# Five pairs of gate tiles instead of four by seven products, and fewer gate steps among the attention units

## What is computed

```python
h = rms_norm(x, g_mix)
proj = h @ w_in                     # A q|k|v, B q|k|v, gate_A, gate_B
y_a = chunk_band_relbias_attention(qa, ka, va, rel_table) @ w_branch_a   # 8 heads
y_b = sliding_window_sink_gqa(rope(qb), rope(kb), vb, sinks) @ w_branch_b  # 8 heads, 2 for keys
g_a, g_b = split(sigmoid(gate_logits + b_gate))   # gate_logits: the last 2 * 1024 columns of proj
x = x + (g_a * y_a + g_b * y_b) @ w_out
x = x + swiglu(rms_norm(x, g_ffn))
```

## Time and profile before

| | |
|---|---|
| median of 3 runs | 2745.28 us (2744.36 to 2747.64) |
| the profiled execution | 2747.8 us |
| its span, first to last instruction | 2745.9 us |
| granted TensorE clock, mean | 0.992 |
| layer 0: projection stage, about | 0 to 293 us |
| layer 0: attention units, about | 299 to 550 us |
| layer 1: attention units, about | 1650 to 1901 us |

### The profile page before, as it was taken

The page is one execution under the profiler, slowest core; times in us unless marked ns, Lnnn a source line. Parts: engine busy times, 40 slices in busy tenths (PEclk is TensorE's granted clock), DMA queues, the critical chain, the costliest instruction groups (busy, mean ns, idle before and its releaser), DMA issues. The chain is left out here.

```text
span 2745.9 us, 37502 instructions
## 1 busy us (share of the span) xinstructions
PE 2688.3 (98%) x13328; PEld 2259.6 (82%) x13328; DVE 1933.4 (70%) x3589; ACT 1173.7 (43%) x2413; POOL 251.5 (9%) x390
## 2 busy tenths in 40 slices
PE   8999999999989999999999999999999999999998
PEld 7788889888878888888778888988887788888887
DVE  6766666654587877767997666666446877786687
ACT  5222577742433333344552227776324333333444
POOL 0000301055200000000000002111450000000000
PEclk8999999999999999999999999999999999999999
DMA  2333433153223222376423334322530322333843
GB/s 96 142 119 105 147 94 94 47 187 132 85 92 115 96 92 104 115 238 195 145 90 116 119 120 132 94 92 75 188 131 29 125 93 103 112 115 114 273 127 123
DMA packets 182295, 330.37 MB, mean 120 GB/s; under 512 B 16992, under 2 KB 62304, under 8 KB 181856
## 3 DMA queue, kind: packets, MB, share of 16 engines
q1 hardware_dynamic: 171968, 301.24, 33.0%
q10 hardware_dynamic: 10144, 26.74, 2.9%
HBM read 235.12 MB, written 92.80 MB: 119 GB/s over the span
## 5 line engine op out<-in xcount | busy, mean ns | idle before, releaser
L1112 PE MATMUL ps<-op_hi,up_hi 128*128 128x512 f32 x1232 | 481.8, 391 | 12.8 <-issue 4.9
L1113 PE MATMUL ps<-op_lo,up_hi 128*128 128x512 f32 x1232 | 480.7, 390 | 0.0
L1114 PE MATMUL ps<-op_hi,up_lo 128*128 128x512 f32 x1232 | 480.6, 390 | 0.0
L1112 PE MATMUL ps<-in_hi,up_hi 128*128 128x512 f32 x728 | 287.9, 396 | 14.9 <-DVE up_lo L2116 11.4
L1751 ACT ACTIVATE up_hi<-up_raw 128x512 fp32r<-128x512 f32 x264 | 165.0, 630 | 294.3 <-PE ps L1114 274.2
L1114 PE MATMUL ps<-in_hi,up_lo 128*128 128x512 f32 x728 | 286.1, 393 | 0.0
L1113 PE MATMUL ps<-in_lo,up_hi 128*128 128x512 f32 x728 | 286.1, 393 | 0.0
L1112 PEld LDWEIGHTS ps<-op_hi,up_hi 128*128 128x128 f32 x1232 | 231.9, 188 | 64.2 <-DVE up_lo L2523 8.5
L1114 PEld LDWEIGHTS ps<-op_hi,up_lo 128*128 128x128 f32 x1232 | 232.1, 188 | 48.6
L1113 PEld LDWEIGHTS ps<-op_lo,up_hi 128*128 128x128 f32 x1232 | 232.1, 188 | 47.9
L1082 POOL CAST w_hi<-w_raw 128x256 fp32r<-128x256 f32 x192 | 82.9, 474 | 1819.0 <-DMA w_raw<-w_lin 1237.9
(11 more groups left out here) (244 smaller groups left out, 5527.9 us busy)
## 6 DMA issues: line engine op xcount, KB each, us to landing
up_raw<-w_gu SPq DMA_DIRECT2D x44, 1024.0 KB, 5.1
act_raw<-ff_saved SPq DMA_DIRECT2D x154, 256.0 KB, 2.8
w_quarter<-w_lin SPq DMA_DIRECT2D x52, 512.0 KB, 4.5
w_raw<-w_lin SPq DMA_DIRECT2D x48, 512.0 KB, 3.9
ff_saved<-ff_block SPq DMA_DIRECT2D x88, 256.0 KB, 2.0
ff_saved<-ff_mix SPq DMA_DIRECT2D x66, 256.0 KB, 2.0
gated<-gates_saved SPq DMA_DIRECT2D x32, 512.0 KB, 4.1
stage<-in_saved SPq DMA_DIRECT2D x48, 256.0 KB, 2.8
```

The costliest lines, as they stand in the source:

```text
L1112: pe.matmul(out, w1, x1, start=first, stop=False, skip_group_check=True)
L1113: pe.matmul(out, w1, x0, start=False, stop=False, skip_group_check=True)
L1114: return pe.matmul(out, w0, x1, start=False, stop=last, skip_group_check=True)
```

## The change

One more pair of gate tiles is computed in the projection stage by seven products: 14 pairs instead of 13 for each layer. Six gate tiles instead of eight are left for plain computing, twelve halves instead of sixteen. Eight steps still stand before the first unit and two halves behind the last, so 10 x 8 - 8 = 72 steps instead of 14 x 8 - 8 = 104 stand among the units. `FILL_A` sums to 22 instead of 26 in group 0 and to 6 instead of 8 in each of the other groups; `FILL_B` is 12, 7, 7 and 6 instead of 14, 14, 14 and 12. Everything else follows from these numbers.

```diff
-IN_GATES = 4
+IN_GATES = 5
 GATE_TILES = 2 * (KT - IN_GATES)
 LIN_TILES = 2 + 4 * GROUPS + 3 * KT + KT
 TILES = GATE_TILES + 2 * KT
@@
-FILL_A = ((3, 3, 3, 2, 2, 2, 2, 1, 1, 1, 1, 1, 1, 1, 1, 1), (1, 1, 1, 1, 1, 0, 1, 0, 1, 0, 0, 0, 1, 0, 0, 0))
-FILL_B = (14, 14, 14, 12)
+FILL_A = ((3, 2, 2, 2, 2, 2, 1, 1, 1, 1, 1, 1, 1, 1, 1, 0), (1, 1, 1, 1, 0, 0, 1, 0, 0, 0, 0, 0, 1, 0, 0, 0))
+FILL_B = (12, 7, 7, 6)
```

## The result

The kernel after the change takes 2765.07 us (median of 4 runs, 2763.81 to 2766.94), the one before 2746.46 us (median of 4). The ratio is 1.0066, with a 95% interval from 1.005 to 1.0082: slower by 18.6 us. The forecast was 2752.5 us with a range up to 2760.5, so the sign was right and the size was not. The profiled execution took 2764.56 us, its span is 2762.8 us, 16.9 more than that of before.

What follows compares the result with a forecast made beforehand. PE was taken as the bound, until ACT or DVE is waited for; 19.04 us added less 15.45 returned gives +3.6 a layer, +7.2 for two: 2752.5 us, range 2745.5 to 2760.5.

Steps and rivals of the forecast that it cites:

- The added pair: Projection stage: one more pair of gate tiles costs 19.04 us for each layer, its ACT and DVE work hidden.
- A of group 0 and of groups 1 to 3: A phases of the attention units: removed steps return 2.4 us in group 0, 2.7 in the other three together, each layer.
- B of group 3: Last B phase of the attention units: six removed steps return in full, 3.6 us a layer, bounds 2.9 to 3.8.
- B of groups 1 and 2: Two B phases of the attention units: seven removed steps each return 3.1 and 3.5 us a layer, ACT limiting.
- rival (b): B phases: ACT and DVE close up worse than thought, every return at its low bound, +17.7 us, 2763 us; chance 0.13.
- B of group 0: First B phase of the attention units: two removed steps return 0.15 us a layer, bounds 0 to 1.2.
- Rival (c): B phases of groups 1 to 3: more PE gaps lower the clock, 24 us for two layers, 2776 us; chance 0.02.
- GpSimd: Among the units: two tiles fewer on POOL slow DVE less, freeing at most some tenths of a microsecond.
- The loads of staged tiles: SP's queue in the attention units: less time between staged load and user, costed at nothing, up to 1 us.

Runs made afterwards that it cites:

- add_only: The kernel before with a 14th projection pair that nobody reads, all 104 gate steps kept; 2787.9 us, ratio 1.0147.
- after_conv: The kernel after the change, with plain query and key conversions of groups 1 to 3 cut to 64 of 512 columns; 2753.52 us, ratio 1.0024.
- after_a26: The kernel after the change, with 26 steps in A of group 0 and 5 instead of 7 in B of groups 1 and 2; 2765.48 us, ratio 1.0063.
- after_light: The kernel after the change, with GpSimd subtracting only 8 of 128 columns for gate tiles 2 and above; 2762.77 us, ratio 1.0053.
- return_only: The kernel after the change without computing its fifth pair of gate tiles, whose gates are read from the fourth; 2727.24 us, ratio 0.9927.
- before_light: The kernel before, with GpSimd subtracting only 8 of 128 columns for gate tiles 2 and above; 2748.51 us, ratio 1.0002.

## Why the prediction was right and wrong

**The added pair: right.** 19.04 us a layer was read and 19.04 measured; its ACT and DVE work stayed hidden. Only add_only's 41.7 us is above twice that, and its excess stands partly in the units.

**A of group 0 and of groups 1 to 3: right within 0.4 and 0.8 us,** 2.1 for 2.4 and 2.3 or 1.9 for 2.7.

**B of group 3: right in kind, 0.3 us too low.** Six steps returned 3.93 us, 0.655 each, above my high bound of 3.8. The 0.60 came from a unit that had gaps of its own.

**B of groups 1 and 2: the mechanism was right, the fill was mis-sized.** The first step returned 0.7 us in each, as said. For the rest I took ACT at 91% of the units from r = 3 on; the windows of after from r = 3 show 16.77 of 19.36 and 16.63 of 19.16 us, 87%:

```profile
427.38:446.74 19.36, 17.27 (x131) 15.15 (x129) 15.44 (x61) 16.77 (x63) 3.26 (x5) 1.00 0.34 107
483.84:503.00 19.16, 17.24 (x131) 15.25 (x129) 15.20 (x62) 16.63 (x63) 4.20 (x8) 1.00 0.40 120
```

That is the 86% of the burst of group 0 again, the low bound, which rival (b) had taken. (The sum used 17.9 us for both groups; for group 2 its own 16.41 us gives 18.0.) The trace had one measured fill for a stretch in which TensorE waits for conversions, and I chose a better one by argument. 0.04 of fill is 0.8 us a phase; ACT's own work also grew by half a microsecond in the first. This term is 2.6 us a layer, over half of the miss (in layer 1, 0.7 of it is the third fall). after_conv shows the cause: with less for ACT and DVE to do, the same steps return 3.0 and 3.8 us.

**B of group 0: right at full clock, wrong as measured.** "A step taken out of such a place returns nothing": the idle time grew by just the step, and where the clock stayed and GpSimd was out of the way (after_a26, layer 0) the phase returned 0.17 us. What failed is the next step: its lower bound of zero. I held idle time to be free, and it brought a half-clock stretch of 3.4 us, and the phase lost 1.4 us in both layers. The stretch cost 1.5 to 1.6 us where nothing stood in its shadow (30.88 against 32.46 us within one trace of after_a26; 31.29 against 32.83 in after_light), and 0.4 in after_conv, where it took the place of a wait at r = 8. In after GpSimd's split would have lengthened that wait by some 0.9 us (an estimate, 1.76 - 0.89), so that 0.7 to 1.5 us a time is the clock's. Rival (c) had the mechanism, but looked for it in half of all B phases, at 24 us, and put 0.02 on it. There it speaks against itself: the gaps of the earlier trace rows (second row) at full clock were taken as proof that gaps do no harm, while the change made the longest one over half as long again. In B of group 1 of layer 1 a third fall made the phase 26.20 instead of 25.48 us. Three falls are 2.1 to 3.7 us of the 16.4.

**The sum.** Without the falls the growth is 12.7 to 14.3 us, and 7.2 was forecast: both errors point the same way, and without the falls the time would have been 2758 to 2760 us, just inside the range. Rival (b)'s +17.7 us was closest to the measured +18.6, and partly by luck: for layer 0 its bounds fit B of groups 1 and 2 (4.4 for 4.0 us) and were 2.5 us too low for the A phases and B of group 3, and it knew no fall.

**GpSimd: wrong in direction.** I wrote that fewer tiles help a little. Fewer they are, but one split moved from A into B of group 0, beside the conversions. It did not lengthen the wait at the transposes (1.91 us with, 1.92 without). At full clock the phase took 31.3 us with a shortened split in it and 30.9 with none, and the waits at r = 8 (0.89, 1.32, 1.76 us) put the whole split at some 0.9 us; in after, where the clock fell before r = 8, it shows as nothing. By the Trainium skill (GPSIMD Engine Reference, Specifications) GpSimd and VectorE contend for SBUF when VectorE reads two inputs; the row of 1.12 us agrees.

**The loads of staged tiles: up to 1 us was too low a bound,** though it did not bear on the result. In return_only, add_only and before_light such a load took 4.4 to 5.2 us instead of 2.7 and TensorE waited 1.8 to 2.3 us behind it; after shows none of these waits. Why these loads were slow is open.

**What stays open.** Why the clock falls behind a 1.9 us wait in one layer and not in the other, and why it fell four times in the units with no wait over 0.9 us before it. The Trainium skill (TensorE: Matmul & The Clock Gate, Part 1) describes an activity monitor that runs free of the kernel's start; that would make such falls a matter of phase, and no run here can show it. Between the units, before and after both show a few such stretches (before at 796.9, 1401.0 and 2128.0 us), one more after, which I didn't pursue.

## What to carry to other kernels

Filler work is worth its time only where the engine is full; where it waits, a step removed becomes idle time, and on TensorE a longer idle time can cost more than the step did. So before moving work out of a stage, move it within: take fill steps from phases in which TensorE is full and put them where it waits (here 2.4 us with the work unchanged), look whether the engine still waits there, and price a waiting stage's return by a fill that its trace shows, with a lower bound below zero.

## What the runs showed of the hardware

In the units of the 15 traces the granted clock fell to 0.50 nineteen times. Fifteen of the falls stand at the end of a wait of TensorE of 1.54 to 1.92 us, as in after, where it was busy for about half of the time before (2.58 of 4.70 us). Four stand behind shorter waits, 0.9 us at most, with TensorE busy for 3.42 to 3.70 of the 4.70 us before. The clock stayed there for 3.4 us, and once for 6.8, and came back by itself. Eleven waits of 1.54 to 2.25 us had no fall behind them. Behind a wait of 1.21 us at the place of the two falls of after, with 2.79 of 4.10 us busy, it did not fall in either layer of before:

```profile
350.00:354.10 4.10, 2.79 (x18) 2.42 (x19) 3.92 (x14) 3.95 (x12) 0.00 (x0) 1.00 0.20 64
```

A mean clock of 0.990 against 0.992 and a page with nines in every slice hide all of it: only windows of a few microseconds show it.
